# The scans of a hybrid encoder trunk: where the rows of cumulated sums come from, and which engine adds the two directions

## The reference

```python
def ssd_chunked(xs, dt, a, bm, cm):               # chunks of 128 positions: c = 4
    X = (xs * dt[..., None]).reshape(b, c, t, g, e, p)
    a_cs = jnp.cumsum((dt * a).reshape(b, c, t, g, e), axis=2)
    ...
    seg = a_cs[:, :, :, None] - a_cs[:, :, None, :]
    decay = jnp.exp(jnp.where(lower, seg, -jnp.inf))
    cb = jnp.einsum('bclgn,bcsgn->bclsg', Cc, Bc)
    y_diag = jnp.einsum('bclsge,bcsgep->bclgep', cb[..., None] * decay, X)
    x_to_end = X * jnp.exp(a_cs[:, :, -1:] - a_cs)[..., None]
    states = jnp.einsum('bcsgn,bcsgep->bcgepn', Bc, x_to_end)
    ...
    y_off = jnp.einsum('bclgn,bcgepn->bclgep', Cc, s_in) * jnp.exp(a_cs)[..., None]
    return (y_diag + y_off).reshape(b, s, h, p)
```

## Time and profile before

| | |
|---|---|
| median of 3 runs | 1684.28 us (1684.26 to 1684.72) |
| the profiled execution, its own time | 1684.64 us |
| its span in the profile | 1682.9 us |
| busy in the span: PE, DVE, ACT, POOL | 1659.0, 1001.9, 679.8, 687.4 us |
| granted TensorE clock | 1.0 |

### The profile page before, as it was taken

The page is one execution under the profiler, slowest core; times in us unless marked ns, Lnnn a source line. Parts: engine busy times, 40 slices in busy tenths (PEclk is TensorE's granted clock), DMA queues, the critical chain, the costliest instruction groups (busy, mean ns, idle before and its releaser), DMA issues.

```text
span 1682.9 us, 20420 instructions
## 1 busy us (share of the span) xinstructions
PE 1659.0 (99%) x8004; PEld 1316.8 (78%) x8004; DVE 1001.9 (60%) x1387; ACT 679.8 (40%) x932; POOL 687.4 (41%) x339
## 2 busy tenths in 40 slices
PE   7999999999999999999999999999999999999999
PEld 5777787878778888888877777788777788888887
DVE  5589859778774545422236898596788654545100
ACT  5445553344443333332244555533543433333221
POOL 3432223233445555554443222232334455555443
PEclk9999999999999999999999999999999999999999
DMA  5532111212223232322224221112123223222233
GB/s 167 129 96 74 62 63 63 76 63 64 87 88 100 88 100 88 100 92 94 91 88 126 85 73 63 63 63 76 63 66 96 89 88 100 89 100 90 93 99 107
DMA packets 43231, 147.34 MB, mean 88 GB/s; under 512 B 5152, under 2 KB 5920, under 8 KB 43136
## 3 DMA queue, kind: packets, MB, share of 16 engines
q1 hardware_dynamic: 42752, 145.28, 26.9%
q0 software_dynamic: 384, 0.75, 0.4%
HBM read 143.17 MB, written 2.85 MB: 87 GB/s over the span
## 4 chain that ended last, share of the span: by engine, by line
PE 89%; DVE 6%; issue 2%; ACT 1%; POOL 1%; DMA 0%; SPq 0%; DVEq 0%
PE banks L1080 27%; PE banks L1082 26%; PE banks L1081 26%; PE banks L1172 2%; PE banks L1151 2%; PE banks L1160 2%; PE banks L1255 1%; DVE sb_w_lo L747 1%; PE banks L1268 1%; PE banks L1227 1%; PE banks L1131 1%; DVE sb_e L822 1%; PE banks L1241 1%; PE banks L1211 0%; DVE sb_squares L735 0%
## 5 line engine op out<-in xcount | busy, mean ns | idle before, releaser
L360 POOL TENSOR_TENSOR sb_w_lo<-sb_w_raw,sb_w_hi 128x1024 fp32r<-128x1024 f32 x202 | 490.4, 2428 | 633.1 <-ACT sb_w_hi L453 633.1
L1080 PE MATMUL banks<-sb_h_hi,sb_w_hi 128*128 128x512 f32 x1360 | 558.2, 410 | 16.1 <-POOL sb_w_lo L360 10.7
L453 ACT ACTIVATE sb_w_hi<-sb_w_raw 128x1024 fp32r<-128x1024 f32 x258 | 272.6, 1057 | 671.4 <-PE banks L1082 665.1
L1082 PE MATMUL banks<-sb_h_hi,sb_w_lo 128*128 128x512 f32 x1360 | 537.3, 395 | 0.0
L1081 PE MATMUL banks<-sb_h_lo,sb_w_hi 128*128 128x512 f32 x1360 | 537.1, 395 | 0.0
L1080 PEld LDWEIGHTS banks<-sb_h_hi,sb_w_hi 128*128 128x128 f32 x1360 | 256.5, 189 | 99.5 <-issue 36.9
L1081 PEld LDWEIGHTS banks<-sb_h_lo,sb_w_hi 128*128 128x128 f32 x1360 | 256.9, 189 | 61.8 <-issue 6.9
L1082 PEld LDWEIGHTS banks<-sb_h_hi,sb_w_lo 128*128 128x128 f32 x1360 | 256.5, 189 | 60.1
L1045 DVE TENSOR_TENSOR banks<-banks,sb_rstd 128x512 f32<-128x512 f32 x88 | 61.5, 699 | 144.0 <-PE banks L1082 135.7
L1080 PE MATMUL banks<-sb_ff_hi,sb_w_hi 128*128 128x512 f32 x352 | 138.9, 395 | 0.0
L1082 PE MATMUL banks<-sb_ff_hi,sb_w_lo 128*128 128x512 f32 x352 | 138.9, 395 | 0.0
(11 more groups left out here) (199 smaller groups left out, 2326.9 us busy)
## 6 DMA issues: line engine op xcount, KB each, us to landing
sb_w_raw<-w_in SPq DMA_DIRECT2D x88, 512.0 KB, 3.4
sb_w_raw<-w_up SPq DMA_DIRECT2D x88, 512.0 KB, 3.3
sb_w_raw<-w_out SPq DMA_DIRECT2D x32, 512.0 KB, 3.4
sb_w_raw<-w_down SPq DMA_DIRECT2D x32, 512.0 KB, 3.3
sb_bias_t<-bias_rows SPq DMA_DIRECT2D x16, 448.0 KB, 6.0
sb_w_raw<-w_down SPq DMA_DIRECT2D x16, 384.0 KB, 3.0
sb_x_stream<-x_t SPq DMA_DIRECT2D x4, 512.0 KB, 6.7
out_t<-sb_x_stream SPq DMA_DIRECT2D x8, 256.0 KB, 3.5
```

Of the source, the lines that this page charges most:

```text
L360: g.tensor_tensor(WLO[:, n % 2, :], W[:, n % 2, :], WHI[:, n % 2, :].bitcast(F32), ALU.subtract).then_inc(w_lo.handle, 1)
L453: sc.activation(WHI[:, n % 2, :], W[:, n % 2, :], ACT.Copy).then_inc(w_hi.handle, 1)
L1080: mm(out, whi, hhi, start=start, stop=False)
L1082: return mm(out, wlo, hhi, start=False, stop=stop)
```

## The change

The spread rows no longer come from TensorE. ScalarE writes the rows of sums to SBUF, and their exponentials beside them (`ER`); SP stores both in DRAM once in each layer (`store_rows`). For every head SP then reads the two rows back, repeated over the 128 partitions, right into the head's buffer (`head_rows`, 512 KB), and for every pair the exponentials, 64 partitions to a head, in two transfers of 192 KB (`pair_exps`). Both stand in SP's list behind the load of a weight block. VectorE subtracts and bounds in one operation, which takes a column as its scalar, so it needs eight of them for a head (2 directions, 4 chunks of 128 elements). ScalarE's exponential for each head's `EA` is gone. GpSimd adds the directions of all heads, so `within` has one product for a chunk and head, and it waits for GpSimd's addition of the odd head. There are four buffers for the heads instead of three; the selecting columns, `CS` and their waits are gone.

```diff
-    HEAD_E = (E[:, 0, :, :], E[:, 1, :, :], SQ[:, :, :])
+    HEAD_E = (E[:, 0, :, :], E[:, 1, :, :], SQ[:, :, :], rm["spread"][:, 0:16:15, :])
...
+        def store_rows():
+
+            sp.wait_ge(*cs_row.at(1))
+            sp.dma_start(sum_rows[0, :, :], T[0:2 * DIR, 0, :]).then_inc(rows_stored.handle, 16)
+            sp.wait_ge(*cs_exp.at(1))
+            sp.dma_start(sum_rows[1, :, :], ER[0:2 * DIR, :]).then_inc(rows_stored.handle, 16)
+
+        def head_rows(h):
+
+            grp, n = h // 8, h % 8
+            if h == 0:
+                sp.wait_ge(*rows_stored.at(32))
+                sp.wait_ge(*at_pv.at(UNITS))
+            if n % 4 == 2:
+                sp.wait_ge(*st_mm.at(6 * grp + 6))
+            if h == 3:
+                sp.wait_ge(*cb_mm.at(1))
+            if h >= 4:
+                sp.wait_ge(*y_mm.at(2 * ((h - 4) // 2) + 2))
+            rows = bass.AP(sum_rows.tensor, h * SEQ, [[0, P], [DIR * SEQ, 2], [1, SEQ]])
+            sp.dma_start(head_e(h), rows).then_inc(rows_landed[h % 4].handle, 16)
+
+        def pair_exps(t):
+
+
+            if t >= 2:
+                sp.wait_ge(*y_read.at(t - 1))
+            for d in range(2):
+                rows = bass.AP(sum_rows.tensor, (2 * DIR + DIR * d + 2 * t) * SEQ + (P, 0)[d], [[SEQ, 2], [0, 64], [1, SEQ - P]])
+                sp.dma_start(EA[:, t % 2, d, :], rows).then_inc(ea_landed[t % 2].handle, 16)
...
+                slot = pos - POS["sc", 0]
+                if slot == 4:
+                    store_rows()
+                if slot - 2 in ROWS_AT:
+                    head_rows(ROWS_AT[slot - 2])
+                if slot - 1 in PAIR_AT:
+                    pair_exps(PAIR_AT[slot - 1])
...
-                if s in ROWS_AT and ROWS_AT[s] % 2 == 0:
+                if s in ROWS_AT:
                     add_directions(ROWS_AT[s])
...
-                    act.wait_ge(*seg_read.at(h + 1))
-                    if h >= 4:
-                        act.wait_ge(*y_read.at(h // 2 - 1))
-                    sc.activation(EA[half, (h // 2) % 2, :, :].rearrange("p d l -> p (d l)"),
-                                  BANK[half, 2:4, :].rearrange("p b s -> p (b s)")[:, P:P + 768], ACT.Exp).then_inc(ea_done.handle, 1)
...
-                    sc.activation(CS[0:64, :], BANK[0:64, 2, :], ACT.Copy).then_inc(cs_hi.handle, 1)
+                    sc.activation(ER[0:64, :], BANK[0:64, 2, :], ACT.Exp).then_inc(cs_exp.handle, 1)
...
         def seg(h):
-            grp, n = h // 8, h % 8
-            dve.wait_ge(*ab_mm.at(h + 1))
...
-            columns = AS[:, :, h:h + DIR + 1:DIR].rearrange("p c d -> p d c").unsqueeze(3).to_broadcast([P, 2, QT, P])
-            v.tensor_tensor(head_e(h).rearrange("p d (c l) -> p d c l", l=P),
-                            BANK[:, 2:4, :].rearrange("p d (c l) -> p d c l", l=P), columns, ALU.subtract).then_inc(seg_read.handle, 1)
-            dve.wait_ge(*seg_read.at(h + 1))
-            v.tensor_scalar(head_e(h), head_e(h), 80.0, None, ALU.min).then_inc(seg_done.handle, 1)
+            dve.wait_ge(*rows_landed[h % 4].at(16 * (h // 4 + 1)))
+
+            for d in range(2):
+                for c in range(QT):
+                    at = slice(P * c, P * c + P)
+                    ins = v.tensor_scalar(head_e(h)[:, d, at], head_e(h)[:, d, at], AS[:, c, column(d, h):column(d, h) + 1], 80.0,
+                                          ALU.subtract, ALU.min)
+            ins.then_inc(seg_done.handle, 1)
...
-            dve.wait_ge(*ea_done.at(2 * t + 2))
+            dve.wait_ge(*ea_landed[t % 2].at(32 * (t // 2 + 1)))
...
-                if k == KT // 2 and head is not None:
-                    row_sums(head)
...
         def within(t):
 
-            pe.wait_ge(*gs_done.at(t + 1))
-            pe.wait_ge(*g_done.at(2 * t + 2))
+            pe.wait_ge(*gs_done.at(2 * t + 2))
...
-                for h, d in ((2 * t, 0), (2 * t + 1, 0), (2 * t + 1, 1)):
+                for h in (2 * t, 2 * t + 1):
                     half = 64 * (h % 2)
                     ins = mm(BANK[half:half + 64, 6 + t % 2, P * c:P * c + P], XT[:, c, 64 * (h % 8):64 * (h % 8) + 64],
-                             head_e(h)[:, d, P * c:P * c + P], start=d == 0, stop=d == h % 2)
-                    if c == QT - 1 and d == h % 2:
+                             head_e(h)[:, 0, P * c:P * c + P], start=True, stop=True)
+                    if c == QT - 1:
                         ins.then_inc(y_mm.handle, 1)
```

More of the change, by code:

```diff
@@ L195, in build_trunk @@
                 ("x_tok", 40, [P, QT, 512], F32), ("s_in", 48, [P, 2, 3, SEQ], F32), ("b_tok", 60, [P, QT, P], F32),
-                ("cs", 62, [P, SEQ], F32R), ("exp_cs", 64, [P, 2, 2, 384], F32), ("cb", 70, [P, 2, SEQ], F32),
+                ("exp_rows", 62, [P, SEQ], F32), ("spread", 32, [P, 16, SEQ], F32), ("exp_cs", 64, [P, 2, 2, 384], F32), ("cb", 70, [P, 2, SEQ], F32),
                 ("e", 74, [P, 2, 2, SEQ], F32), ("mh_sc", 82, [P, 4, SEQ], F32R), ("ml_sc", 90, [P, 4, SEQ], F32R),
@@ L233, in build_trunk @@
     x_stored = sem("x_stored")
-    sel_done, eps_done = sem("sel_done"), sem("eps_done")
+    eps_done = sem("eps_done")
+    rows_stored = sem("rows_stored", 32)
+    rows_landed = [sem(f"rows_landed{i}", 64) for i in range(4)]
+    ea_landed = [sem("ea_landed0", 128), sem("ea_landed1", 128)]
     bias_mm, bias_row = sem("bias_mm"), sem("bias_row")
@@ L270, in head_e @@
     def head_e(h):
-        return HEAD_E[h % 8 % 3]
+        return HEAD_E[h % 4]
     def par(col, n=1):
@@ L710, in setup @@
         def setup():
-            dve.wait_ge(con_landed.handle, 16)
-            v.tensor_tensor(SEL[:, :], con["ident"][:, 0:64], con["ident"][:, 64:128], ALU.add).then_inc(sel_done.handle, 1)
             for r in range(2):
@@ L855, in state_in @@
                 return
[L856 to L857 removed]
+            dve.wait_ge(*(t_read.at(4) if grp else rows_stored.at(32)))
             col = 64 + column(d, 8 * grp)
@@ L1103, in block_of, with tile @@
                 ins.then_inc(w_used.handle, 1)
-        def tile(kind, i, width=P, head=None):
+        def tile(kind, i, width=P):
             for k in range(KT):
-                if k == KT // 2 and head is not None:
-                    row_sums(head)
                 block_of(kind, i, k, width)
@@ L1227, in chunk_state @@
             mm(bank(4 + d), BT[:, c, :], SQ[:, j % 2, :], start=True, stop=True).then_inc(st_mm.handle, 1)
-        def row_sums(h):
-            if h:
-                pe.wait_ge(*ea_done.at(h))
-                pe.wait_ge(*seg_read.at(h))
-            else:
-                pe.wait_ge(*cs_lo.at(1))
-                pe.wait_ge(*cs_col.at(1))
-            if h % 8 == 0:
-                pe.wait_ge(*tok_copied.at(5 * (h // 8) + 1))
-            if h == 0:
-                pe.wait_ge(sel_done.handle, 1)
-            for d in range(2):
-                ins = mm(bank(2 + d), SEL[:, column(d, h):column(d, h) + 1].to_broadcast([P, P]), CS[:, :], start=True, stop=True)
-            ins.then_inc(ab_mm.handle, 1)
         def within(t):
-            pe.wait_ge(*gs_done.at(t + 1))
-            pe.wait_ge(*g_done.at(2 * t + 2))
+            pe.wait_ge(*gs_done.at(2 * t + 2))
             if t % 4 == 0:
@@ L1270, in from_states, with output_first @@
             ins.then_inc(yo_mm.handle, 1)
-        def output_first(m, head):
+        def output_first(m):
             s, b = weights("o1", m), tile_bank("o1", m)
             for k in range(KT):
-                if k == KT // 2 and head is not None:
-                    row_sums(head)
                 at = slice(P * k, P * k + P)
@@ L1345, in _ @@
                 if kind == "o1":
-                    output_first(i, ROWS_AT.get(s))
+                    output_first(i)
                 else:
-                    tile(kind, i, head=ROWS_AT.get(s))
+                    tile(kind, i)
                 if s == 0:
```

28 lines of the change are left out of this document (7 added, 21 removed).

## The result

The changed kernel takes 1704.85 us (median of 4 runs, 1704.47 to 1707.29) where the kernel before took 1684.3 on the same chip (1684.26 to 1684.72): a ratio of 1.0124, with a 95% interval of 1.0107 to 1.0142. It is slower by 20.6 us; forecast were 22.7. The profiled execution took 1707.29 us with a span of 1705.5, where before it was 1684.64 with 1682.9, so the two profiles differ by 22.6.

The account below looks back on a forecast made before the run. VectorE's chain, lengthened by GpSimd, and TensorE were taken to run without slack at the same pace. Terms of 3.3 and 8.25 us a layer, 23.1 in two, on 1684.64 gave 1707 us, slower; range 1670 to 1737.

Parts of the forecast that it names:

- the turns: VectorE operations on SBUF wait for the GpSimd instruction under way, subtraction from PSUM doesn't; a 512-element GpSimd addition costs 1.15 us.
- the sum: Per layer 3.3 us in the first group and 8.25 in the second; 23.1 us over two layers, giving 1707.4 us.
- TensorE's removed work: Spreading products (15.0 us) and a third of the products in `within` (10.1) go, 24.8 us net, with no gain expected.
- The eight operations: VectorE's short subtractions take 0.20 us each, 1.6 a head, gaining 0.25; bounds 1.3 to 2.3 us a head.
- The turns of the first group: Heads 0 to 7: VectorE +4.2 us net, pair 3's products start 3.9 late and end 3.3 late.
- The turns of the second group: Heads 8 to 15, with GpSimd's gates and square sums too: +8.25 us a layer, 2.2 of it before pair 7.
- the items between: Between heads 9 and 15: head 10 +0.3 us, head 11 +0.2, head 12 -0.25, head 13 +2.15, head 14 -0.25.
- the net of head 15: VectorE meets the backward addition and square sums, less costs paid before and a gate no longer ahead of weighing: +1.2 us.
- head 13's, 2.15: VectorE meets a backward addition (0.95), a gate (1.25) and the new addition (1.1), less 0.9 paid before and 0.25: +2.15 us.
- Nothing on the path in my sum: Head rows land 3.4 to 6.9 us after issue, hidden by one VectorE iteration; the transfers add no time.
- a sign against itself: The prediction would be wrong if VectorE waits in the stage for DMA.
- two engines for each pair's exponentials: Rival: pair transfers with outermost count 2 take 8.9 us and delay the subtraction; 20 to 40 us, about 1735; chance 0.14.

## Why the prediction was right, and where it was not

**The total.** 1707 was forecast and 1704.85 measured, slower by 1.2%, by the mechanism that the forecast names. That it came so near is in part luck: the turns were put too high, and the clock, which is not in the sum, made up for it (below). The shift came in like amounts in both layers: TensorE's product with the sums of squares stands at 447.52 after and 436.46 before, 11.06 us later, where 11.55 a layer was the sum.

**TensorE's removed work.** It went (192 products, L1241 is gone), and none of it showed: right. But its busy time fell by 13.5 us, where 24.8 were worked out. The work that is left ran slower in the stretches after its waits; that is where the difference of 11.3 has to lie, since the products are fewer by as many as was counted. The kernel without row sums and with even additions held back, whose clock is 0.999 over the span, is busy for 1646.2, near 1659.0 - 15.0 = 1644.0. The prediction had no term for the clock; the next paragraphs show what it is worth on the path.

**The eight operations.** 1.6 us a head was worked out by overlapping starts, 1.66 measured where nothing is in the way. The estimate of 1.0 us by the formula of the Trainium skill's page VectorE: DVE Perf Modes, section "The TRN2 errata", is too low here.

**The turns of the first group.** Worked out was that pair 3's products start 3.9 us late. They started at 324.22, which is 2.5 after the earlier trace rows; the stage had begun 0.8 earlier. After head 7's weighing, which ended at 321.91, they waited 2.3, as worked out. Heads 1, 2, 4, 5 and 7, the five that the sum had named, showed the turns (2.67, 2.67, 2.47, 2.44 and 2.44 us for 1.66), each 0.8 to 1.0 long. The pair's products ended 1.65 late (325.25 for 323.60), where +3.3 was worked out. The tenth product after the pair then started 3.20 late: nine products took 3.75 us at the lowered clock, where they took 2.20 before. So the clock gave half of what the sum had put down to turns.

```profile
323.60 0.50 PE L1080 MATMUL banks<-sb_h_hi,sb_w_hi 128*128 128x512 f32 x1
...
325.80 0.39 PE L1080 MATMUL banks<-sb_h_hi,sb_w_hi 128*128 128x512 f32 x1
```

```profile
325.25 0.68 PE L1104 MATMUL banks<-sb_h_hi,sb_w_hi 128*128 128x512 f32 x1
...
329.00 0.39 PE L1104 MATMUL banks<-sb_h_hi,sb_w_hi 128*128 128x512 f32 x1
```

The first fence is the kernel before, the second the changed one.

**The turns of the second group.** From head 8's subtraction to the end of head 15's weighing it was 67.69 us (355.05 to 422.74) for 63.95: +3.74, where 8.25 - 2.2 = 6.05 was worked out. Head 9 took 4.21 us and head 15 5.58, as the mechanism says; the items between and the net of head 15 were too high. The largest is head 13's, 2.15: its eight operations took 2.41, 0.75 too long. From its start to head 14's it was 1.82 more than before (8.74 for 6.92), and 1.17 of that is head 14's wait for its rows, which the sum did not have at all. The last pair then waited 2.3 after the weighing, as worked out (+2.2). Head 8 began 3.2 late (355.05 for 351.87); 3.2 + 3.7 + 2.2 are 9.1 of the 11.06. The rest is the half clock: ten products after the pair took 4.37 us (426.95 to 431.32) where they took 2.43 before (417.82 to 420.25). With the 1.55 after pair 3 the clock is 3.5 us of this layer's 11.06.

**The transfers: the step that failed.** "Nothing on the path in my sum" was wrong, and the right total hid it. VectorE did wait for rows, which the prediction had named as a sign against itself. The waits were short (4.3 us in all), because the turns had already made VectorE late. With the turns out of the way they grew to 12.0 us, and the kernel was still at 1700. The prediction had the right row for it, as a rival: two engines for each pair's exponentials. It took the rival as another outcome, with a price to add; it was a second bound at the same height. Its estimate of 8.9 us for the pair's transfers is somewhat short: from their issue at 257.85 they were under way until 268 at least, 10 us. What it missed is what that does to the head rows: those of `sb_squares`, issued after a pair's exponentials, landed in 9.3 us with the two-engine transfers and in 5.0 without, where 3.4 to 6.9 were taken. That they queue behind the exponentials on the two engines is the likely reading; no view shows the engines one by one. Head 2, which the prediction named as the one with the least time (5.4 us), waited longest, 3.39 once the turns were gone.

**Why removing the odd additions alone did not give what the sum had for them.** Without the odd heads' additions the sum would have lost all of the first group's 3.3, and in the second group 0.55 and 1.1 for the new additions and 2.2 for pair 7: 7.2 us a layer, 14.3 in two. Undone with the two-engine transfers they gave 3.9 in two layers; undone with the transfers on sixteen, 16.9, the clock's part included. So their total was about right, and they were not the only bound.

**What is open.** The part of the loss that is the clock alone was not taken apart by a run; the 3.5 us a layer are read from one trace, and the lowered clock is itself a consequence of the waits. It does not order the kernels: the mean clock over the span was 0.993 in the profiled run of 1689.25 us (all additions held back, sixteen engines), but 0.996 in that of 1700.35 (no additions, two engines). The changed kernel with sixteen engines and all its additions in place stayed at 1705.4 although the span of its profile is 1701.1; its runs reach from 1702.87 to 1706.31, and a gain of some 2 us can't be excluded.

## What to carry to other kernels

Where two chains bound a stage at the same height, undoing one part at a time shows for each that it is innocent: try the parts in pairs before a suspect is let go, and read in each single run what the freed engine waits for next. A VectorE operation that is moved from PSUM to SBUF can be held up by GpSimd where it was not before, so GpSimd's list has to be looked at with it. Here the transfers on all engines and the odd additions undone took a loss of 1.2% down to 0.25%, and only then a few waits on GpSimd made a gain of 0.45% of it. Look at the outermost count of every transfer, of those with slack too: here two such transfers went with a landing of the next rows in 9.3 us instead of 5.0.

## What the runs showed of the hardware

- TensorE's granted clock was 0.50 (425 to 429) after a wait of 6.03 us and a mean of 0.81 (291.5 to 300) and 0.66 (324.2 to 328) in the stretches after waits of 3.64 and 2.21 us, and back at 1.00 at 436. At the lower level products of 128 columns follow by 0.21 us where they follow by 0.11 at full clock. After the wait of 2.21 us the pair's products still ran at full clock, and only those from 325.25 on at half.
- Short VectorE operations in SBUF (1.66 us for eight undisturbed) took 2.67 beside the rest of one GpSimd addition and 5.58 and 6.61 beside three and four GpSimd instructions in a row: at head 15 one of 1.04 us and right behind it one of 2.43, beside a GpSimd instruction of 2.40, so that hardly a short operation got through between the two. The Trainium skill's page SBUF — State Buffer, section "Who interferes with whom", says that for the VectorE modes that use both ports the engine that issues first keeps the shared ports for the whole instruction and the other is blocked; these rows agree with it. Eight that read PSUM took 2.15 us beside a GpSimd addition (267.53) and without one (273.91), and none of the 256 took more than 0.35.
- Two transfers of 192 KB with an outermost count of 2 kept the DMA share at 0.13 to 0.15 from 262 to 268; two of the same size with a count of 64 landed in 6.3 us (median), and the rows in `sb_squares` then landed in 5.0 instead of 9.3.
